# Weight remainders of a two-layer decoder trunk by accumulating transfers instead of GpSimd subtractions

## The chip, the cores and the metric

One core of one Trainium2 chip runs the whole program. The metric is device time in microseconds, from the first to the last instruction of the launch. The kernel before was timed three times: 1368.78, 1369.29 and 1370.32 us, so the median is 1369.29 us.

## The reference

Everything is float32. The sequence has 512 positions of width 1024, and there are two layers. Each layer is a mixer and a SwiGLU feed-forward, and both are wrapped as `x <- LayerNorm(alpha * x + f(x))`:

```python
for layer in range(DEPTH):                                   # DEPTH = 2
    if layer % 2 == 0:
        h = conv_sgu_mixer(x, ...)                           # 1024 -> 2048 in, 1024 -> 1024 out
    else:
        h = dilated_attention_mixer(x, positions, ...)       # 1024 -> 9216 q/k/v, 3 groups x 8 heads x 128
    x = layer_norm(DN_ALPHA * x + h, ln_g[layer, 0], ln_b[layer, 0])
    x = layer_norm(DN_ALPHA * x + swiglu(x, w_gate, w_up, w_down), ln_g[layer, 1], ln_b[layer, 1])

def swiglu(x, w_gate, w_up, w_down):                         # hidden width 2816
    return (jax.nn.silu(x @ w_gate) * (x @ w_up)) @ w_down
```

What matters here is the weights: 236 pieces of 512 KB (128 partitions x 1024 float32), called slabs, are read once each and multiplied with activations that stay on the chip.

## The kernel before

**Products in three passes.** TensorE multiplies in the format fp32r, which keeps fewer bits than float32. To keep float32's precision each factor is split in two: the rounded value (`_hi`) and the remainder (`_lo` = value - rounded value), and a product is made as hi*hi + hi*lo + lo*hi. So each slab of weights needs three things before TensorE can finish with it: its load, its rounded copy and its remainder.

**The ring of slabs.** Loads, rounded copies and remainders each have RING = 4 places; slab n uses place n % 4. The steps of a plain slab are:

- SyncE's queue loads it into `stage` (`load_view`); it waits until the remainder of slab n-4 is made, since that reads the old contents of the place.
- ScalarE (ACT) copies `stage` to `w_hi`, which rounds it (`split_high`, L1201); it waits for the load and until TensorE has used slab n-4 (`w_used`). It then counts up `w_hi_ready`.
- GpSimd (Pool) subtracts, `w_lo = stage - w_hi` (`split_low`, L618); it waits for `w_hi_ready` and counts up `w_lo_ready`.
- TensorE (PE) waits for `w_lo_ready` (`slab_ready`) and multiplies: `columns` (L712 to L714) for q, k and the columns behind a norm, `tokens` (L734 to L736) for down and output projections, L1129 to L1131 for v.

Each of these queues runs in the order in which the code issues, without a planner. ACT's order around the change is written out: a slab's rounding stands in front of other work of that stage, as the rounding of the hidden activations (L1457), the copies of q and k out of PSUM (L1525), of v (L1589) and the exponentials (L1536).

**The stages**, with the slab numbers that the text uses:

| slabs | stage | who makes the remainder before |
|---|---|---|
| 0 to 23 | layer 0, mixer in and out | Pool |
| 24 to 67 | layer 0, gate and up (4 plain ones, then units) | Pool 3 and VectorE 1; units VectorE |
| 68 to 89 | layer 0, down projection | Pool |
| 90 to 161 | layer 1, q, k, v | Pool |
| 162 to 169 | layer 1, output projection | Pool |
| 170 to 213 | layer 1, gate and up | as layer 0 |
| 214 to 235 | layer 1, down projection | Pool |

**Where three slabs are wanted at once.** Down and output projections go slab by slab over all four token tiles (`whole_rows`), 24 products of 512 columns each. The last three slabs go tile by tile instead (`finish_tiles`), so that the LayerNorm of tile 0 can start early. It therefore waits for all three remainders at its start: slabs 87 to 89, 167 to 169 and 233 to 235. The last of the three can be rounded only when slab n-4 has been used, which leaves one slab's products between that and the start of `finish_tiles`.

**Behind a norm** (`columns_behind_norm`) the first four slabs of the next stage are multiplied in two rounds, tokens 0 to 255 of all four and then tokens 256 to 511 of all four, and only the second round releases their places, one every 24 short products. Slab 94 is the first one after the four of layer 1's q and k.

Of the kernel before, what the change touches and what calls it, by code (L numbers as in the profile page):

```python
# [10 lines left out]
ACT = mybir.ActivationFunctionType  # L11
ALU = mybir.AluOpType
# [28 lines left out]
RING = 4  # L41


N_IN, N_OUT, N_UP, N_DOWN, N_ATT = 16, 8, 2 * KF, KF, 72
S_IN = 0
S_OUT0 = S_IN + N_IN
S_UP0 = S_OUT0 + N_OUT
S_DOWN0 = S_UP0 + N_UP
S_ATT = S_DOWN0 + N_DOWN
S_OUT1 = S_ATT + N_ATT  # L50
S_UP1 = S_OUT1 + N_OUT
# [55 lines left out]
def trunk(nc, x, positions, ev_w_in, ev_conv_w, ev_conv_b, ev_conv_ln_g, ev_conv_ln_b, ev_sgu_ln_g,  # L107
# [3 lines left out]
    with ctx:  # L111
        def sb(name, shape, dt=F32, scope=ctx):
            return scope.enter_context(nc.sbuf_tensor(name, shape, dt))

        def sem(name):
            return ctx.enter_context(nc.semaphore(name))
# [6 lines left out]
        w_stage = [stage[:, j, :] for j in range(RING)]  # L123
        w_hi = [sb(f"w_hi{j}", [P, SLAB], F32R) for j in range(RING)]
        w_lo = [sb(f"w_lo{j}", [P, SLAB], F32R) for j in range(RING)]
# [91 lines left out]
        w_loaded = [sem(f"w_loaded{j}") for j in range(RING)]  # L217
        w_hi_ready = sem("w_hi_ready")
        w_lo_ready = sem("w_lo_ready")
        w_used = sem("w_used")  # L220
        x_loaded = [sem(f"x_loaded{i}") for i in range(TILES)]
        ident_loaded = sem("ident_loaded")
# [139 lines left out]
        def plain(slab):  # L362

            return slab - sum(min(max(slab - up - RING, 0), N_UP - RING) for up in (S_UP0, S_UP1))

        def unit_stage(up, par):

            first = (up + 2 * par) % RING
            return stage[:, first, :], stage[:, first + 1, :], stage[:, first:first + 2, :].rearrange(
                "p a (b n) -> p (a b) n", n=512)  # L370
# [53 lines left out]
        def v_slab(turn, k):  # L424

            return S_ATT + turn * TURN_SLABS + QK_SLABS + k
# [85 lines left out]
        def _(sp):  # L512
            def load_view(slab, turns, view):

                slot = slab % RING
                behind_units = [(up // S_UP1, slab - up - N_UP) for up in (S_UP0, S_UP1)
                                if up + N_UP <= slab < up + N_UP + RING]
                if behind_units:
                    layer, j = behind_units[0]
                    sp.wait_ge(d_lo_set if j % 2 else s4_set, layer * UNITS + UNITS - 1 + j // 2)  # L520
                elif slab >= RING:
                    sp.wait_ge(w_lo_ready, plain(slab - RING) + 1 + RING * turns)
                dst = w_stage[slot][:, :].rearrange("p (k n) -> p k n", k=view.shape[1])
                sp.dma_start(dst, view).then_inc(w_loaded[slot], 16)

# [83 lines left out]
        @block.gpsimd  # L609
        def _(pool):  # L610
            pool.memset(ones[:, :], 1.0 / CONV_CH).then_inc(ones_set, 1)
            pool.memset(eps[:, :], EPS).then_inc(ones_set, 1)
            pool.memset(a_pad[:, :, 0:PAD], 0.0).then_inc(pad_set, 1)

            def split_low(slab, turns=0):

                pool.wait_ge(w_hi_ready, plain(slab) + 1 + RING * turns)
                pool.tensor_tensor(w_lo[slab % RING][:, :], w_stage[slab % RING][:, :],  # L618
                                   w_hi[slab % RING][:, :].bitcast(F32), ALU.subtract).then_inc(w_lo_ready, 1)

            def add_shift(e, i):

                for half in range(2):
                    pool.wait_ge(x_scaled, SCALED_PARTS * e + min(2 * i + half + 1, SCALED_PARTS))
                    xh = x_res[:, i, half * 512:(half + 1) * 512]
                    pool.tensor_tensor(xh, xh, norm_b[:, half * 512:(half + 1) * 512], ALU.add).then_inc(x_normed, 1)

            def norm(e, following):

                if e < 3:  # L630
                    split_low(following)
                add_shift(e, 0)
                add_shift(e, 1)
                if e < 3:
                    split_low(following + 1)
                add_shift(e, 2)
                if e < 3:
                    split_low(following + 2)
                    if e in (0, 2):
                        keep_x(e, following)  # L640
                    else:
                        split_low(following + 3)

            def keep_x(e, up):

                pool.wait_ge(w_used, plain(up))
                pool.wait_ge(xt_set, 2 * TILES * (e + 1) + 4)
                for half in range(2):
                    k = slice(half * KH, (half + 1) * KH)
                    pool.tensor_tensor(x_kept[:, k, :], xt_hi[:, k, 0:HALF].bitcast(F32), xt_lo[:, k, 0:HALF].bitcast(F32),  # L650
                                       ALU.add).then_inc(x_kept_set, 1)

            for slab in range(S_UP0):
                split_low(slab)
                if slab == 17:
                    pool.wait_ge(acc_set, 1)
                    pool.wait_ge(chunk_summed, 1)
                    pool.tensor_tensor(tap_sum[:, 0, :], acc[:, 0, :], acc[:, 2, :], ALU.add).then_inc(pair_summed, 1)
                for n, c, w in conv_taps(slab):
                    if w == dve_taps[c]:  # L660
                        continue
                    m = n - 1 - c
                    pool.wait_ge(tap_product, n + 1)
                    if m:
                        pool.wait_ge(tap_added, m)
                    pool.tensor_tensor(tap_sum[:, c, :], tap_sum[:, c, :], mixed[:, m % 2, :], ALU.add
                                       ).then_inc(tap_added, 1)
                    if w == CONV_WIDTH - 1:
                        pool.wait_ge(sum_begun, c + 1)
                        pool.wait_ge(tap_added, m + 1)  # L670
                        pool.tensor_tensor(acc[:, c, :], acc[:, c, :], tap_sum[:, c, :], ALU.add
                                           ).then_inc(chunk_summed, 1)
            norm(0, S_UP0)

            def feed_forward(down, e):
                with pool.Fori(0, N_DOWN // RING) as t:
                    for j in range(RING):
                        split_low(down + j, t)
                for slab in range(down + N_DOWN // RING * RING, down + N_DOWN):
                    split_low(slab)  # L680
                norm(e, down + N_DOWN)

            feed_forward(S_DOWN0, 1)
            with pool.Fori(0, N_ATT // RING - 1) as t:
                for j in range(RING):
                    split_low(S_ATT + RING + j, t)
            for slab in range(S_OUT1, S_UP1):
                split_low(slab)
            norm(2, S_UP1)
            feed_forward(S_DOWN1, 3)  # L690
# [4 lines left out]
        @block.tensor  # L695
        def _(pe):
            def slab_ready(slab, turns=0):
                pe.wait_ge(w_lo_ready, plain(slab) + 1 + RING * turns)

            def columns(slab, bank, tiles=(0, TILES)):  # L700

# [95 lines left out]
            for c in range(CC):  # L797
                slab = S_IN + 2 * c
# [12 lines left out]
            for s in range(4):  # L811
                slab = S_IN + 8 + s
# [20 lines left out]
            for c in range(CC):  # L833
                slab = S_IN + 12 + c
# [355 lines left out]
        def _(act):  # L1190
            def split_high(slab, turns=0):

                act.wait_ge(w_loaded[slab % RING], 16 * (slab // RING + 1) + 16 * turns)
                behind_units = [(up // S_UP1, slab - up - N_UP) for up in (S_UP0, S_UP1)
                                if up + N_UP <= slab < up + N_UP + RING]
                if behind_units:
                    layer, j = behind_units[0]
                    act.wait_ge((a1_used, s12_used, s3_used, d_used)[j], (layer + 1) * UNITS - (j == 3))
                elif slab >= RING:
                    act.wait_ge(w_used, plain(slab - RING) + 1 + RING * turns)  # L1200
                act.activation(w_hi[slab % RING][:, :], w_stage[slab % RING][:, :], ACT.Copy).then_inc(w_hi_ready, 1)  # L1201

            def x_high(e, i):
                for half in range(2):
# [123 lines left out]
            for i in range(TILES):  # L1328
                act.activation(v_tok[:, i, :], v_tok[:, i, :], ACT.Identity, bias=shift[:, i:i + 1],
                               scale=rstd[:, i:i + 1]).then_inc(v_set, 1)  # L1330
# [227 lines left out]
            for turn in range(TURNS):  # L1558
# [20 lines left out]
                for k in range(V_SLABS):  # L1579
                    g, a = divmod(k, 4)  # L1580
                    slab = v_slab(turn, k)
# [64 lines left out]
        def _(dve):  # L1646
# [252 lines left out]
            def feed_forward(layer, up, e):  # L1899
# [3 lines left out]
                def low_plain(slab):  # L1903

                    dve.wait_ge(w_hi_ready, plain(slab) + 1)
                    dve.wait_ge(w_lo_ready, plain(slab))
                    dve.tensor_tensor(w_lo[slab % RING][:, :], w_stage[slab % RING][:, :],
                                      w_hi[slab % RING][:, :].bitcast(F32), ALU.subtract).then_inc(w_lo_ready, 1)

# [362 lines left out]
```

## Time and profile before

| | |
|---|---|
| runs | 1368.78, 1369.29, 1370.32 us; median 1369.29 us |
| profiled execution | span 1369.0 us from its first to its last instruction; nothing else of its time is given |
| TensorE (PE), busy | 1355.4 us, 99% |
| VectorE (DVE), busy | 887.1 us, 65% |
| ScalarE (ACT), busy | 615.3 us, 45% |
| GpSimd (POOL), busy | 451.1 us, 33% |
| DMA | 133.52 MB on SyncE's queue, 33.3% of 16 engines' span |

The shares of the four engines are averages over very different stages. For a change at one point of the ring the columns to look at are the start times of the instructions of one slab on each engine: they tell how long before TensorE wanted a remainder it was there. PE's records are pipelined: one product of 512 columns is shown with 0.39 us, but the next one starts 0.227 us behind it (24 of them make 5.44 us), so starts are read, not durations.

### The profile page before, as it was taken

To read this page: it belongs to the slowest core of one execution; us is meant where nothing else is said; L and a number is where in the kernel's file an instruction comes from. 1 tells how busy PE (TensorE), PEld (TensorE's weight loads), DVE (VectorE), ACT (ScalarE), POOL (GpSimd) and SP (SyncE) were. 2 spreads that over 40 slices of the span, in tenths; PEclk is the share of its full clock that TensorE was granted. 3 is DMA by queue.
4 is the path that set the end of the run, shared out by engine and by line. 5 is a ranking of instruction groups with operands and counts; after the bars stand their busy time and mean duration, and the time that the engine had idled before them with its cause. 6 is when DMAs were issued, how large, how long until landed. Compare 5 with 4: busy or idle time off the path is not lost.

```text
span 1369.0 us, 20672 instructions
## 1 busy us (share of the span) xinstructions
PE 1355.4 (99%) x8121; PEld 1208.5 (88%) x8121; DVE 887.1 (65%) x1122; ACT 615.3 (45%) x959; POOL 451.1 (33%) x218
## 2 busy tenths in 40 slices
PE   8999999999999999999999999999999999999997
PEld 7887899999988889888888888888889999998886
DVE  3997698888856355677433665724159888885445
ACT  4465555555542454333433434434255555554233
POOL 4785600000054454344443332444260000005443
PEclk9999999999999999999999999999999999999999
DMA  9323223343453323332442322254122334335321
GB/s 269 93 94 92 63 78 108 92 122 92 112 167 95 105 62 93 93 93 84 132 124 67 88 82 73 77 164 130 47 62 78 107 92 122 92 113 164 96 74 62
DMA packets 181961, 138.72 MB, mean 101 GB/s; under 512 B 8789, under 2 KB 162153, under 8 KB 181896
## 3 DMA queue, kind: packets, MB, share of 16 engines
q1 hardware_dynamic: 175272, 133.52, 33.3%
q10 hardware_dynamic: 6624, 4.29, 1.3%
q8 instruction: 45, 0.74, 0.2%
q14 instruction: 20, 0.16, 0.0%
HBM read 133.56 MB, written 4.24 MB: 101 GB/s over the span
## 4 chain that ended last, share of the span: by engine, by line
PE 97%; DVE 1%; DMA 1%; ACT 1%; SPq 0%; issue 0%; DVEq 0%
PE pq L940 10%; PE pq L939 10%; PE pq L937 10%; PE pq L712 9%; PE pq L714 9%; PE pq L713 9%; PE pq L734 8%; PE pq L735 8%; PE pq L736 8%; PE pq L1130 3%; PE pq L1131 3%; PE pq L1129 3%; PE pq L1108 1%; PE pq L1067 1%; PE pq L1080 1%; PE pq L1101 1%
## 5 line engine op out<-in xcount | busy, mean ns | idle before, releaser
L618 POOL TENSOR_TENSOR w_lo<-stage,w_hi 128x1024 fp32r<-128x1024 f32 x154 | 374.5, 2441 | 873.9 <-ACT w_hi L1201 873.8
L1201 ACT ACTIVATE w_hi<-stage 128x1024 fp32r<-128x1024 f32 x156 | 161.6, 1056 | 238.2 <-PE pq L736 164.8
L712 PE MATMUL pq<-xt_hi,w_hi 128*128 128x512 f32 (+1 forms) x624 | 228.4, 366 | 0.5 <-DVE xt_lo L1653 0.4
L714 PE MATMUL pq<-xt_hi,w_lo 128*128 128x512 f32 (+1 forms) x624 | 225.2, 361 | 0.0
L713 PE MATMUL pq<-xt_lo,w_hi 128*128 128x512 f32 (+1 forms) x624 | 225.1, 361 | 0.0
L940 PE MATMUL pq<-xt_hi,w_lo 128*128 128x256 f32 x632 | 178.9, 283 | 0.0
L939 PE MATMUL pq<-xt_lo,w_hi 128*128 128x256 f32 x632 | 178.9, 283 | 0.0
L937 PE MATMUL pq<-xt_hi,w_hi 128*128 128x256 f32 x632 | 178.8, 283 | 0.0
L712 PEld LDWEIGHTS pq<-xt_hi,w_hi 128*128 128x128 f32 x624 | 117.9, 189 | 19.5 <-DVE xt_lo L1653 1.2
L714 PEld LDWEIGHTS pq<-xt_hi,w_lo 128*128 128x128 f32 x624 | 117.8, 189 | 18.0
L937 PE MATMUL pq<-xs_hi,w_hi 128*128 128x256 f32 x472 | 133.6, 283 | 0.0
L939 PE MATMUL pq<-xs_lo,w_hi 128*128 128x256 f32 x472 | 133.6, 283 | 0.0
L940 PE MATMUL pq<-xs_hi,w_lo 128*128 128x256 f32 x472 | 133.6, 283 | 0.0
L713 PEld LDWEIGHTS pq<-xt_lo,w_hi 128*128 128x128 f32 x624 | 117.9, 189 | 17.1
L937 PEld LDWEIGHTS pq<-xt_hi,w_hi 128*128 128x128 f32 x632 | 121.3, 192 | 0.1
L939 PEld LDWEIGHTS pq<-xt_lo,w_hi 128*128 128x128 f32 x632 | 121.3, 192 | 0.1
L940 PEld LDWEIGHTS pq<-xt_hi,w_lo 128*128 128x128 f32 x632 | 121.3, 192 | 0.0
L2032 DVE TENSOR_TENSOR xs_lo<-ht,xs_hi 128x512 fp32r<-128x512 f32 x26 | 63.4, 2440 | 67.7 <-ACT xs_hi L1457 67.7
L937 PEld LDWEIGHTS pq<-xs_hi,w_hi 128*128 128x128 f32 x472 | 90.6, 192 | 0.0
L939 PEld LDWEIGHTS pq<-xs_lo,w_hi 128*128 128x128 f32 x472 | 90.6, 192 | 0.0
L940 PEld LDWEIGHTS pq<-xs_hi,w_lo 128*128 128x128 f32 x472 | 90.6, 192 | 0.0
L734 PE MATMUL pq<-w_hi,xs_hi 128*128 128x512 f32 x208 | 81.0, 389 | 0.0
(261 smaller groups left out, 2808.4 us busy)
## 6 DMA issues: line engine op xcount, KB each, us to landing
stage<-in_od_w_qkv_dram SPq DMA_DIRECT2D x72, 512.0 KB, 3.9
stage<-in_ffn_w_gate_dram SPq DMA_DIRECT2D x44, 512.0 KB, 4.9
stage<-in_ffn_w_up_dram SPq DMA_DIRECT2D x44, 512.0 KB, 3.9
stage<-in_ffn_w_down_dram SPq DMA_DIRECT2D x44, 512.0 KB, 3.5
stage<-in_ev_w_in_dram SPq DMA_DIRECT2D x16, 512.0 KB, 5.7
stage<-in_ev_w_out_dram SPq DMA_DIRECT2D x8, 512.0 KB, 3.6
stage<-in_od_w_out_dram SPq DMA_DIRECT2D x8, 512.0 KB, 3.9
x_res<-in_x_dram SPq DMA_DIRECT2D x4, 512.0 KB, 6.2
```

The costliest lines, as they stand in the source:

```text
L618: pool.tensor_tensor(w_lo[slab % RING][:, :], w_stage[slab % RING][:, :], w_hi[slab % RING][:, :].bitcast(F32), ALU.subtract).then_inc(w_l ...
L712: pe.matmul(o, hi[:, k, :], x_hi, start=(k == 0), stop=False)
L713: pe.matmul(o, hi[:, k, :], x_lo, start=False, stop=False)
L714: last = pe.matmul(o, lo[:, k, :], x_hi, start=False, stop=(k == KD - 1))
L734: pe.matmul(o, t_hi[:, tile * P:(tile + 1) * P], hi, start=first, stop=False)
L735: pe.matmul(o, t_hi[:, tile * P:(tile + 1) * P], lo, start=False, stop=False)
L736: return pe.matmul(o, t_lo[:, tile * P:(tile + 1) * P], hi, start=False, stop=end)
L937: pe.matmul(o, hi[:, k, :], x_block[0][:, k, :], start=(first and k == 0), stop=False, skip_group_check=True)
L939: pe.matmul(o, hi[:, k, :], x_block[1][:, k, :], start=False, stop=False, skip_group_check=True)
L940: last = pe.matmul(o, lo[:, k, :], x_block[0][:, k, :], start=False, stop=(k == KH - 1), skip_group_check=True)
L1201: act.activation(w_hi[slab % RING][:, :], w_stage[slab % RING][:, :], ACT.Copy).then_inc(w_hi_ready, 1)
L2032: dve.tensor_tensor(lo, ht[:, k, :], hi.bitcast(F32), ALU.subtract).then_inc(ht_set, 1)
```

## The change

For 120 slabs the remainder is no longer a subtraction on Pool. ACT writes the rounded slab twice, once as before into `w_hi` and once with its sign turned into `w_lo`; only then does it count up `w_hi_ready`. Pool issues a DMA that adds `stage` onto `w_lo` (`accum_op=ALU.add`), from on-chip memory to on-chip memory, 512 KB, so that `w_lo` becomes stage - rounded slab. Its landing is counted on one new semaphore for each place of the ring, and all who waited for `w_lo_ready` of such a slab wait for that: PE's `slab_ready` and SyncE's load of slab n+4.

The 120 slabs are those from the first down projection on (68 to 89, 94 to 169, 214 to 235). The four slabs behind each norm (90 to 93, 170 to 173), everything before slab 68 and the units stay as they are.

```diff
+        w_lo_landed = [sem(f"w_lo_landed{j}") for j in range(RING)]
...
+        def lo_done(slab, turns=0):
+
+            if by_transfer(slab):
+                return w_lo_landed[slab % RING], 16 * sum(by_transfer(n) and not in_units(n) for n in range(slab % RING, slab + 1, RING))
+            return w_lo_ready, sum(not by_transfer(n) and not in_units(n) for n in range(slab + 1)) + turns * RING
...
+        def by_transfer(slab):
+
+            return S_DOWN0 <= slab and not any(n <= slab < n + RING for n in (S_ATT, S_UP1))
...
-                    sp.wait_ge(w_lo_ready, plain(slab - RING) + 1 + RING * turns)
+                    sp.wait_ge(*lo_done(slab - RING, turns))
...
                 pool.wait_ge(w_hi_ready, plain(slab) + 1 + RING * turns)
+                if by_transfer(slab):
+                    pool.dma_start(w_lo[slab % RING][:, :], w_stage[slab % RING][:, :], accum_op=ALU.add
+                                   ).then_inc(lo_done(slab)[0], 16)
+                    return
                 pool.tensor_tensor(w_lo[slab % RING][:, :], w_stage[slab % RING][:, :],
                                    w_hi[slab % RING][:, :].bitcast(F32), ALU.subtract).then_inc(w_lo_ready, 1)
...
-                pe.wait_ge(w_lo_ready, plain(slab) + 1 + RING * turns)
+                pe.wait_ge(*lo_done(slab, turns))
...
-                act.activation(w_hi[slab % RING][:, :], w_stage[slab % RING][:, :], ACT.Copy).then_inc(w_hi_ready, 1)
+                high = act.activation(w_hi[slab % RING][:, :], w_stage[slab % RING][:, :], ACT.Copy)
+                if by_transfer(slab):
+                    high = act.activation(w_lo[slab % RING][:, :], w_stage[slab % RING][:, :], ACT.Copy, scale=-1.0)
+                high.then_inc(w_hi_ready, 1)
```

Pool's loops over the slabs of the down projections and of the attention projections become straight code. On Pool, from the last two instructions of layer 0's first norm to the end of the program, this stands in the queue before (`w_lo<-stage,w_hi` is the subtraction, `x_res<-x_res,norm_b` the adds of the LayerNorm's shift):

```order
L676 UNCONDITIONAL_BRANCH
L676 ISA
L618 TENSOR_TENSOR w_lo<-stage,w_hi 128x1024 [waits w_hi_ready]
L617 REGISTER_ALU
...
L676 COMPARE_AND_BRANCH
L618 TENSOR_TENSOR w_lo<-stage,w_hi 128x1024 [waits w_hi_ready] x3
L626 TENSOR_TENSOR x_res<-x_res,norm_b 128x512 [waits x_scaled] x4
L618 TENSOR_TENSOR w_lo<-stage,w_hi 128x1024 [waits w_hi_ready]
```

and in its place after the change:

```order
L634 DMA w_lo<-stage 128x1024 [waits w_hi_ready] x22
L637 TENSOR_TENSOR w_lo<-stage,w_hi 128x1024 [waits w_hi_ready]
L645 TENSOR_TENSOR x_res<-x_res,norm_b 128x512 [waits x_scaled] x4
L637 TENSOR_TENSOR w_lo<-stage,w_hi 128x1024 [waits w_hi_ready]
L645 TENSOR_TENSOR x_res<-x_res,norm_b 128x512 [waits x_scaled] x2
L637 TENSOR_TENSOR w_lo<-stage,w_hi 128x1024 [waits w_hi_ready] x2
L634 DMA w_lo<-stage 128x1024 [waits w_hi_ready] x76
```

The 22 subtractions of the down projection have become transfers, the four around the norm have stayed where they stood, and the next 76 slabs are transfers again.

On ACT, behind the norm of layer 0 and around slabs 94 and 95, the queue before is (`qk<-pq` copies q or k out of PSUM, `xt_hi<-pq` rounds the turned activations):

```order
L1201 ACTIVATE w_hi<-stage 128x1024 x2
L1206 ACTIVATE xt_hi<-pq 128x16x32 x4
L1525 ACTIVATE qk<-pq 128x512 x2
L1201 ACTIVATE w_hi<-stage 128x1024 x2
L1525 ACTIVATE qk<-pq 128x512 x2
```

and after the change:

```order
L1216 ACTIVATE w_hi<-stage 128x1024 x2
L1224 ACTIVATE xt_hi<-pq 128x16x32 x4
L1543 ACTIVATE qk<-pq 128x512 x2
L1216 ACTIVATE w_hi<-stage 128x1024
L1218 ACTIVATE w_lo<-stage 128x1024
L1216 ACTIVATE w_hi<-stage 128x1024
L1218 ACTIVATE w_lo<-stage 128x1024
L1543 ACTIVATE qk<-pq 128x512 x2
```

The first row (slabs 92 and 93) is unchanged; slabs 94 and 95 take four instructions of ACT instead of two, and slab 95's rounding stands behind slab 94's negated copy.

## Rows read from the trace of the kernel before

**Rows 1.** The page: busy us by engine, and the chain that ended last.

```profile
PE 1355.4 (99%) x8121; PEld 1208.5 (88%) x8121; DVE 887.1 (65%) x1122; ACT 615.3 (45%) x959; POOL 451.1 (33%) x218
...
PE 97%; DVE 1%; DMA 1%; ACT 1%; SPq 0%; issue 0%; DVEq 0%
```

**Rows 2.** PE's waits, 376 to 1369 us: us in total, times, longest.

```profile
PE pq L712 <- DVE xt_lo L1653: 0.2, 1, 0.2
PE pq L712 <- issue: 0.2, 1, 0.2
```

**Rows 3.** The page's groups: busy us, mean ns, idle before.

```profile
L618 POOL TENSOR_TENSOR w_lo<-stage,w_hi 128x1024 fp32r<-128x1024 f32 x154 | 374.5, 2441 | 873.9 <-ACT w_hi L1201 873.8
L1201 ACT ACTIVATE w_hi<-stage 128x1024 fp32r<-128x1024 f32 x156 | 161.6, 1056 | 238.2 <-PE pq L736 164.8
```

**Rows 4.** Timeline (start, us, what), one slab of the down projection, four engines.

```profile
401.58 1.06 ACT L1201 ACTIVATE w_hi<-stage 128x1024 fp32r<-128x1024 f32 x1 [3.86 <-PE pq L736]
402.55 0.61 ACT L1457 ACTIVATE xs_hi<-ht 128x512 fp32r<-128x512 f32 x1
...
402.72 2.40 POOL L618 TENSOR_TENSOR w_lo<-stage,w_hi 128x1024 fp32r<-128x1024 f32 x1 [3.04 <-ACT w_hi L1201]
...
403.19 2.48 DVE L2032 TENSOR_TENSOR xs_lo<-ht,xs_hi 128x512 fp32r<-128x512 f32 x1 [2.96 <-ACT xs_hi L1457]
...
406.76 0.39 PE L734 MATMUL pq<-w_hi,xs_hi 128*128 128x512 f32 x1
```

**Rows 5.** Timeline, slab 89 and the start of `finish_tiles`.

```profile
483.18 1.06 ACT L1201 ACTIVATE w_hi<-stage 128x1024 fp32r<-128x1024 f32 x1 [3.86 <-PE pq L736]
...
488.36 0.39 PE L734 MATMUL pq<-w_hi,hr_hi 128*128 128x512 f32 x1
```

**Rows 6.** Timeline, slab 235 and the start of the last `finish_tiles`.

```profile
1338.81 1.06 ACT L1201 ACTIVATE w_hi<-stage 128x1024 fp32r<-128x1024 f32 x1 [3.86 <-PE pq L736]
...
1343.99 0.39 PE L734 MATMUL pq<-w_hi,hr_hi 128*128 128x512 f32 x1
```

**Rows 7.** Timeline, slabs 94 and 95 on ACT, and slab 94's first product.

```profile
527.27 2.01 ACT L1201 ACTIVATE w_hi<-stage 128x1024 fp32r<-128x1024 f32 x2
...
531.86 0.40 PE L712 MATMUL pq<-xt_hi,w_hi 128*128 128x512 f32 x1
```

**Rows 8.** Timeline, slab 68: ACT, VectorE beside it, Pool, its first product.

```profile
378.78 1.05 ACT L1201 ACTIVATE w_hi<-stage 128x1024 fp32r<-128x1024 f32 x1
...
379.04 0.68 DVE L2032 TENSOR_TENSOR hr_lo<-ht,hr_hi 128x512 fp32r<-128x512 f32 x1
...
379.90 10.41 POOL L618 TENSOR_TENSOR w_lo<-stage,w_hi 128x1024 fp32r<-128x1024 f32 x4 [208.92 <-ACT w_hi L1201]
...
384.97 0.40 PE L734 MATMUL pq<-w_hi,hr_hi 128*128 128x512 f32 x1
```

**Rows 9.** The page's DMA issues: count, KB each, median us to landing.

```profile
stage<-in_ffn_w_down_dram SPq DMA_DIRECT2D x44, 512.0 KB, 3.5
...
v_rows<-v_att ACTq DMA_DIRECT2D x2, 1024.0 KB, 6.6
...
out_dram<-x_res SPq DMA_DIRECT2D x3, 512.0 KB, 2.7
```

**Rows 10.** Four slabs of the down projection: busy us by engine, PEclk, DMA share.

```profile
396.00:418.00 22.00, 22.00 (x99) 18.23 (x98) 11.19 (x10) 6.41 (x9) 9.62 (x4) 1.00 0.31 99
```

**Rows 11.** Timeline, the copies of v out of PSUM behind slab 120.

```profile
672.99 1.06 ACT L1201 ACTIVATE w_hi<-stage 128x1024 fp32r<-128x1024 f32 x1 [2.85 <-issue]
...
674.47 2.29 ACT L1589 ACTIVATE v_att<-pq 128x512 f32<-128x512 f32 x4 [0.42 <-DMA far_rows<-st_far]
...
675.97 0.39 PE L1129 MATMUL pq<-w_hi,xt_hi 128*128 128x512 f32 x1
```

**Rows 12.** Two stretches at the program's start, columns as in Rows 10.

```profile
4.90:11.70 6.80, 3.51 (x28) 2.79 (x27) 2.50 (x4) 3.77 (x7) 1.39 (x1) 1.00 1.03 338
11.70:15.10 3.40, 3.20 (x15) 3.20 (x16) 2.55 (x4) 2.34 (x5) 0.97 (x1) 0.51 1.20 294
```

More of the change, by code:

```diff
@@ L364, in plain, with in_units @@
             return slab - sum(min(max(slab - up - RING, 0), N_UP - RING) for up in (S_UP0, S_UP1))
+        def lo_done(slab, turns=0):
+            if by_transfer(slab):
+                return w_lo_landed[slab % RING], 16 * sum(by_transfer(n) and not in_units(n) for n in range(slab % RING, slab + 1, RING))
+            return w_lo_ready, sum(not by_transfer(n) and not in_units(n) for n in range(slab + 1)) + turns * RING
+        def in_units(slab):
+            return any(up + RING <= slab < up + N_UP for up in (S_UP0, S_UP1))
+        def by_transfer(slab):
+            return S_DOWN0 <= slab and not any(n <= slab < n + RING for n in (S_ATT, S_UP1))
         def unit_stage(up, par):
@@ L675, in feed_forward @@
             def feed_forward(down, e):
[L676 to L679, printed above, removed]
+                for slab in range(down, down + N_DOWN):
                     split_low(slab)
@@ L683, in _ @@
             feed_forward(S_DOWN0, 1)
-            with pool.Fori(0, N_ATT // RING - 1) as t:
-                for j in range(RING):
-                    split_low(S_ATT + RING + j, t)
+            for slab in range(S_ATT + RING, S_OUT1):
+                split_low(slab)
             for slab in range(S_OUT1, S_UP1):
@@ L1905, in low_plain @@
                     dve.wait_ge(w_hi_ready, plain(slab) + 1)
-                    dve.wait_ge(w_lo_ready, plain(slab))
+                    dve.wait_ge(*lo_done(slab - 1))
                     dve.tensor_tensor(w_lo[slab % RING][:, :], w_stage[slab % RING][:, :],
```

## The prediction

> **What bounds the kernel now.** I read the page first. TensorE is busy 99% of the span, and the chain of work that ended last is 97% PE [rows 1]. A busy PE alone proves little, since its records overlap, so the second view is that of PE's waits over the stretch in which the change acts, from the first down projection at 376 us to the end: two waits of 0.2 us each, 0.4 us in all [rows 2]. So from there on the end is set by the number of products times their spacing, and whatever makes remainders faster than TensorE wants them is worth at most 0.4 us. Pool's subtractions are nowhere on that path: Pool sits idle 873.8 us waiting for ACT's rounding [rows 3]. The question is only the opposite one: where is a remainder made so shortly before it is wanted that a slower way of making it shows? That is the third view, the timeline of single slabs.
>
> **What is removed.** 120 subtractions of 2.44 us [rows 3], 293 us of Pool. They are hidden behind PE today, so this is worth nothing by itself. One side effect: VectorE's remainder of the hidden activations takes 2.48 us when it overlaps a Pool subtraction [rows 4] and 0.68 us for the same shape just before Pool starts [rows 8]. It gets shorter.
>
> **What is added on ACT.** 120 negated copies. I price them as the rounding, 1.056 us [rows 3]; a pair of such instructions takes 2.01 us [rows 7]. That is 127 us on an engine that is busy 45%. In the down projections the xs_hi rounding behind it starts 1.0 us later, so VectorE starts at 404.2 instead of 403.19; PE wants the result at 406.76. With 2.48 us it would be there at 406.7, with 0.68 us at 404.9: hidden either way, though by 0.1 us only if VectorE stays slow [rows 4]. Where v is copied out of PSUM the negated copy of slab 120 pushes four copies from 674.47 to about 675.5; the first takes 0.6 and PE wants its bank at 675.97, so about 0.2 us are lost, in each of two turns [rows 11]: 0.4 us. The other work behind the roundings (q and k copies, exponentials) goes later by one or two copies; PE has no wait on any of it today [rows 2], and I cost it at 0, with a bound of 2 us over both layers.
>
> **The new step: ACT, issue, transfer, landing.** For a slab whose rounding starts at A the transfer is issued at A + 2.01 + 0.08 (the 0.08 is what Pool needs today to start behind ACT's end, 402.64 to 402.72 [rows 4]). The room for it is the time from there to PE's first product that needs the slab:
>
> - A slab in mid-projection: 401.58 + 2.09 = 403.67. The product at 406.76 begins the slab two before it [rows 4], so it is wanted at 406.76 + 2 x 5.44 = 417.6. Room 14 us. Nothing to pay.
> - The last slab of three `finish_tiles` (89, 169, 235): 483.18 + 2.09 = 485.27, wanted at 488.36 [rows 5]. Room 3.09 us. The last one is 1338.81 and 1343.99, the same 5.18 us apart [rows 6]; slab 169 repeats it.
> - Slab 94, first behind the four of layer 1's q and k: 527.27 + 2.09 = 529.36, wanted at 531.86 [rows 7]. Room 2.50 us. Slab 95 is rounded behind the negated copy of 94, so its issue is at 531.4, but it is wanted 5.4 us behind 94 plus the scores: room over 7.
> - The first slab of each down projection (68, 214): 378.78 + 2.09 = 380.87, wanted at 384.97 [rows 8]. Room 4.10 us, twice.
>
> So six places out of 120 have less than 4.2 us, and what they cost hangs on one number that the trace does not hold: L, the time from issue to landing of an accumulating transfer of 512 KB within on-chip memory.
>
> **Bounds of L.** From below: a store of 512 KB out of on-chip memory lands in 2.7 us; a load of a down slab in 3.5 us; 1024 KB out of on-chip memory in 6.6 us [rows 9]. The new transfer writes 512 KB but has to read two operands of 512 KB, so its reads are like the 1024 KB row, its write like the smaller ones. The engines' own time for one plain pass of 512 KB is 0.31 x 22 / 4 = 1.7 us [rows 10]. A load plus one further pass is 3.5 + 1.7 = 5.2 us. I take 5.5 us, between that and 6.6 and nearer to the first, because Pool's queue issues none in this trace and may need more before the first byte. Ends: 2.7 us, and 3.5 + 6.6 = 10.1 us if reading and writing do not overlap.
>
> The Trainium skill (DMA: Bandwidth & Descriptors, the anatomy of one DMA on the GpSimd path) gives 2.0 us plus the bytes at 436 GB/s, an estimate of 3.2 us here and of 4.4 us if the second operand is added as a second pass. Collectives: The Full Stack (why ReduceScatter is half of AllGather) says that an add in the transfer costs through its two source reads, not through the adding. By 4.4 us the sum would be 1.9 + 3 x 1.3 + 2 x 0.3 = 6.4 us and the time about 1376 us. No row here shows either.
>
> **The sum.** With L = 5.5: slab 94 waits 3.0 us; three ends of projections 2.4 us each, 7.2; two starts 1.4 each, 2.8. That is 13.0 us. At the first four of the six with loads around (89, 169, 68, 214) a load's 1.7 us of engine time [rows 10] can fall beside the transfer, since the load of slab n+4 now goes out just when slab n has landed; between 0 and 1.7 us each, I take 0.4: 1.6 us. With 0.4 for the v copies the sum is 15.0 us. PE has nothing behind these waits to catch up with, so each one moves the end. Against the profile's own 1369.0 us that is 1384.0 us; the median of the runs is 0.3 us above that span, so I forecast 1384 us.
>
> At the ends of L: with 2.7 only slab 94 is late, by 0.2 us, 1369.5 us. With 6.6 it is 4.1 + 10.5 + 5.0 = 19.6, with full collisions (6.8) 1395 us. With 10.1 it is 7.6 + 21.0 + 12.0 = 40.6, 1410 us.
>
> **Rivals.**
>
> *The transfer is short enough (not slower).* If it lands within about 3.1 us of its issue, all of the six but slab 94 keep their time, as the 2.7 us of a plain store allow [rows 9]. Against it: it reads twice what that store reads. Its place is the start of `finish_tiles`, its price is 0.2 to 0.8 us, and it decides from L below 3.4, where the sum is 0.9 + 0.9 = 1.8 us. Time 1369.5 to 1371 us. A real gain would need PE's spacing to shrink; PE is not waiting, and nothing in these rows ties its spacing to Pool.
>
> *The DMA engines become the bound.* A slab of the down projection takes 5.44 us, its load 1.7 us of all engines [rows 10]. If the accumulate holds them longer than 3.7 us, the ring starves everywhere, not in six places. Twice a plain pass is 3.4 us, close to that, which speaks for it; against it, the ring has 14 us of room, so only a mean rate above 100% counts. With 4.7 us of engine time a slab is 1.0 us late in the 44 down slabs and about 0.3 us in the 76 attention and output slabs (6.1 us each, 531.86 to 995.85): 67 us, 1436 us. If all of the 6.6 us were engine time, some 300 us.
>
> *TensorE's clock falls at each stop.* At the program's start PE was busy 3.51 of 6.80 us, and in the 3.40 us behind that the granted clock was 0.51, the level of 1.2 GHz; before it was 1.00, that of 2.4 GHz [rows 12]. A stop of 3 us is comparable with that idle time. If each of the six stops brought such a stretch, 1.7 us more each: 10 us, 1394 us. Against it: the shortest stops are 1.4 us inside long dense stretches.
>
> **Chances.** The forecast as it stands (L between 4 and 7.5 us, no clock loss, 1374 to 1397 us): 0.62. Clock loss on top: 0.12. DMA engines the bound: 0.10. Transfer short enough: 0.16, most of which is no change (0.13) and 0.03 an unforeseen gain. A measurement of this kernel can tell about 0.2%, 2.7 us, from no change, so slower means above 1372 us: 0.84, the first three cases. The range 1370.5 to 1412 us reaches into the short transfers from L = 3.2 us on, about half of that case, and leaves out 0.08 below and 0.10 above.
>
> **What would show it.** In the profile after: Pool's subtractions down from 154 to 34, ACT up by about 127 us, VectorE's L2032 near 0.7 us. PE's waits list a DMA into w_lo with six long waits, the longest at slab 94, three alike and two shorter; PE's waits on anything else stay below 1 us. Issue to landing of w_lo reads 5.5 us, and the DMA share in the down projections rises from 0.31 to about 0.65. The prediction is wrong if L is under 3.4 us, if PE waits at more than about ten slabs, or if the time changes with no DMA in PE's waits.

## The result and the profile after

The changed kernel takes 1389.59 us (median of 4 runs, 1389.0 to 1393.37) against 1369.03 us before: ratio 1.0153, 95% interval 1.0139 to 1.0168, so it is 20.6 us slower. The forecast was 1384 us, with 1370.5 to 1412 as its range. The profiled execution took 1389.0 us, of which 1387.0 are its span, 18.0 more than the span before.

The page after, busy us by engine and the chain that ended last, beside [rows 1]:

```profile
PE 1360.4 (98%) x8121; PEld 1210.4 (87%) x8121; DVE 764.0 (55%) x1122; ACT 730.0 (53%) x1079; POOL 263.9 (19%) x218
...
PE 92%; DMA 3%; ACT 2%; DVE 1%; issue 1%; SPq 0%; ACTq 0%; DVEq 0%
```

The work moved as intended: Pool 187 us less, VectorE 123 us less, ACT 115 us more. No sum of this kind is the limit. What reached the path is the 3% of DMA in the chain, which had 1% before, and 2% of ACT instead of 1%: at the places named below the negated copy and the transfer stand one behind the other in front of PE (e5). PE's waits from 376 us on (columns: us in total, times, longest), beside [rows 2]:

```profile
PE pq L749 <- DMA w_lo<-stage: 7.3, 4, 2.7
PE pq L749 <- DVE ht L2043: 3.7, 1, 3.7
PE pq L727 <- DMA w_lo<-stage: 2.2, 1, 2.2
PE pq L1144 <- ACT v_att L1607: 0.9, 1, 0.9
PE pq L727 <- DVE xt_lo L1671: 0.2, 1, 0.2
PE pq L727 <- issue: 0.2, 1, 0.2
```

The 0.4 us of before have become 14.5 us. By their times the stops are slab 68 (0.8), 89 (2.1), 94 (2.2), 169 (2.7), 214 (3.7), 235 (1.6), and one behind a copy of v (0.9). That is one at each of the six places of the prediction and no other transfer of the 120. The second line names VectorE for slab 214; experiment e6 shows that this is the transfer too.

One of the stops, slab 89, on ACT, Pool and PE (start, us, what), beside [rows 5]:

```profile
481.69 1.06 ACT L1216 ACTIVATE w_hi<-stage 128x1024 fp32r<-128x1024 f32 x1 [2.91 <-PE pq L751]
482.66 1.05 ACT L1218 ACTIVATE w_lo<-stage 128x1024 fp32r<-128x1024 f32 x1
...
484.00 0.86 POOL L634 DMA_DIRECT2D w_lo<-stage  x1 [4.58 <-ACT w_lo L1218]
...
486.64 0.39 PE L751 MATMUL pq<-w_hi,hr_lo 128*128 128x512 f32 x1
489.15 0.47 PE L749 MATMUL pq<-w_hi,hr_hi 128*128 128x512 f32 x1 [2.11 <-DMA w_lo<-stage]
```

ACT's pair takes 2.0 us, Pool issues 0.3 us behind it, and PE goes on 5.15 us behind the issue. The step from one product to the next is 2.51 us instead of 0.23.

How long a transfer takes from issue to landing, all 120 (the first line below) and that of slab 94, with no load beside it (the second):

```profile
DMA to landing us min/median/max: 4.5/6.0/11.4
...
DMA to landing us min/median/max: 4.5/4.5/4.5
```

And the stretches in which TensorE's granted clock was at half rate, with the program's start in front and a stretch of the down projection at the end (columns: busy us by engine, PEclk, DMA share, GB/s), beside [rows 10, 12]:

```profile
11.70:15.10 3.40, 3.40 (x31) 3.40 (x30) 1.61 (x3) 2.66 (x4) 1.45 (x1) 1.00 1.18 286
490.20:493.60 3.40, 3.40 (x10) 2.62 (x9) 0.00 (x0) 0.00 (x0) 0.44 (x1) 0.50 0.78 205
538.00:541.40 3.40, 3.40 (x9) 2.63 (x9) 2.70 (x4) 2.76 (x3) 1.61 (x2) 0.50 1.10 235
1254.80:1258.20 3.40, 2.86 (x7) 2.31 (x8) 1.80 (x3) 2.20 (x3) 0.86 (x1) 0.50 1.03 175
396.00:462.00 66.00, 66.00 (x293) 54.67 (x292) 16.13 (x44) 34.42 (x46) 10.34 (x12) 1.00 0.89 200
```

The three stretches at 0.50 begin just behind the stops at 89 and 94 and at the end of that at 214. In the first two PE starts 8 products in 3.4 us where it starts 15 at full rate (x10 and x9 also count products that only reach into the stretch). Read from the starts of the same products in both traces, the three cost 1.6, 1.6 and 1.3 us, 4.5 us in all. The first line goes the other way: at the program's start this execution had no half-rate stretch, the profiled one of before had one [rows 12], and the changed kernel runs 2.6 us ahead from there. The unusual one of the two is the execution of before: its span was 1369.0 us, while 23 others of the same kernel, run beside e1, had spans of 1366.4 to 1368.4 us, median 1366.8. So the span's 18.0 us are 14.1 us of new waits, 4.5 us of clock and about 2.0 us of late first products behind the stops and small shifts, less 2.6 us at the start. Without these 2.6 us the difference is 20.6 us, as the runs have it.

### The profile page after: what moved, and what is told of

Read it like the earlier page. It is cut to its first block, busy times and chain, and to the rows that moved or that the text cites. A ratio compares the mean times of both kernels' runs of the same rounds, so it can differ in the third digit from the quotient of the medians.

```text
span 1387.0 us, 20627 instructions
## 1 busy us (share of the span) xinstructions
PE 1360.4 (98%) x8121; PEld 1210.4 (87%) x8121; DVE 764.0 (55%) x1122; ACT 730.0 (53%) x1079; POOL 263.9 (19%) x218
## 3 DMA queue, kind: packets, MB, share of 16 engines
q1 hardware_dynamic: 175272, 133.52, 32.1%
q0 software_dynamic: 17280, 62.92, 25.5%
## 4 chain that ended last, share of the span: by engine, by line
PE 92%; DMA 3%; ACT 2%; DVE 1%; issue 1%; SPq 0%; ACTq 0%; DVEq 0%
PE pq L955 9%; PE pq L954 9%; PE pq L952 9%; PE pq L727 9%; PE pq L729 9%; PE pq L728 9%; PE pq L749 8%; PE pq L751 8%; PE pq L750 8%; PE pq L1144 3%; PE pq L1146 3%; PE pq L1145 3%; DMA w_lo<-stage 2%; PE pq L1123 1%; PE pq L1082 1%; PE pq L1095 1%
## 5 line engine op out<-in xcount | busy, mean ns | idle before, releaser
L634 POOL DMA_DIRECT2D w_lo<-stage x120 | 104.9, 874 | 1014.5 <-ACT w_lo L1218 994.5
L1216 ACT ACTIVATE w_hi<-stage 128x1024 fp32r<-128x1024 f32 x156 | 164.9, 1059 | 186.8 <-PE pq L751 129.9
L1218 ACT ACTIVATE w_lo<-stage 128x1024 fp32r<-128x1024 f32 x120 | 126.2, 1052 | 0.0
L637 POOL TENSOR_TENSOR w_lo<-stage,w_hi 128x1024 fp32r<-128x1024 f32 x34 | 82.3, 2427 | 55.3 <-ACT w_hi L1216 55.3
```

Of the source, the lines that this page charges most:

```text
L634: pool.dma_start(w_lo[slab % RING][:, :], w_stage[slab % RING][:, :], accum_op=ALU.add).then_inc(lo_done(slab)[0], 16)
L1216: high = act.activation(w_hi[slab % RING][:, :], w_stage[slab % RING][:, :], ACT.Copy)
L1218: high = act.activation(w_lo[slab % RING][:, :], w_stage[slab % RING][:, :], ACT.Copy, scale=-1.0)
```

## The experiments

Nine kernels, each an edit of the changed kernel. Ratios are against runs of the kernel before on the same chip.

### e1: the six slabs back on Pool

```diff
-            return S_DOWN0 <= slab and not any(...)
+            return slab not in (S_DOWN0, S_ATT - 1, S_ATT + RING, S_UP1 - 1, S_DOWN1, N_SLABS - 1) and S_DOWN0 <= slab and not any(...)
```

> The changed kernel with six slabs (68, 89, 94, 169, 214, 235) given back to Pool; the other 114 remainders are still transfers. Theory (the loss is six landings behind PE's need, plus the half-clock stretches that follow such stops): about 1370 us, PE waits for no DMA into w_lo, one wait of 0.9 us on a v copy may stay, no half-clock stretch between the start and the end of the program. Rival A (the extra 127 us of ACT work costs): stays 5 us or more above before. Rival B (the DMA engines are near full and slow everything): stays above 1380 us, with PE waits at other slabs.

Measured: 1371.03 us, ratio 1.0010 (1.0001 to 1.0019). 114 transfers are left, and 19 of the 20.6 us are gone; 1.8 us are left. PE's waits:

```profile
PE pq L1144 <- ACT v_att L1607: 0.7, 1, 0.7
PE pq L727 <- DVE xt_lo L1671: 0.2, 1, 0.2
PE pq L727 <- issue: 0.2, 1, 0.2
```

No wait on a transfer of the ring, and the granted clock is 1.00 from 15 us to 1363 us. ACT is still busy 722.8 us (before: 615.3), and the DMA share in the down projection is still 0.87. Both rivals fall: neither ACT's extra work nor nearly full DMA engines costs more than those 1.8 us by itself.

### e2: the negated copies without the transfers

```diff
+        def negated(slab):
+            return S_DOWN0 <= slab and not any(...)
...
         def by_transfer(slab):
+            return False
...
-                if by_transfer(slab):
+                if negated(slab):
                     high = act.activation(w_lo[...], w_stage[...], ACT.Copy, scale=-1.0)
```

> ACT writes the 120 negated copies as in the changed kernel, but every remainder is Pool's subtraction, which overwrites them; no transfer. Theory: the negated copies alone cost 0.9 to 1.5 us (the v copies), and up to 0.2 us per down slab if VectorE's slow remainder of the hidden activations (2.48 us beside Pool) now ends behind PE's need: 1370 to 1376 us. Rival A (ACT's work is the loss): near 1389 us. Rival B: 1369 to 1371 us, as no transfer is left.

Measured: 1368.96 us, ratio 0.9999 (0.9990 to 1.0008), under the expected 1370 to 1376. The 120 copies cost nothing that can be measured, and PE has no wait on a v copy. All its waits from 376 us on:

```profile
PE pq L731 <- issue: 0.2, 1, 0.2
PE pq L731 <- DVE xt_lo L1675: 0.2, 1, 0.2
```

So ACT's copy in front of the v copies does not make PE wait by itself.

### e3: only the six slabs as transfers

```diff
-            return S_DOWN0 <= slab and not any(...)
+            return slab in (S_DOWN0, S_ATT - 1, S_ATT + RING, S_UP1 - 1, S_DOWN1, N_SLABS - 1)
```

> Only the six slabs 68, 89, 94, 169, 214, 235 are transfers, the other 114 are Pool's. Theory: most of the loss is back, less what neighbouring transfers add by sharing the engines: waits of 2.1 (94), 1.5 to 2.0 (three ends), 0.6 to 1.5 (two starts), about 9.5 us, and some 1.6 us for each of about three half-clock stretches: 1378 to 1386 us, centre 1382. Issue to landing 4.5 us, 5 with a load beside it. Rivals A and B (ACT's total work, full DMA engines): 1370 us or less.

Measured: 1381.57 us, ratio 1.0091 (1.0076 to 1.0107), in the middle of what was expected. PE's waits:

```profile
PE pq L749 <- DMA w_lo<-stage: 7.5, 4, 2.6
PE pq L727 <- DMA w_lo<-stage: 2.2, 1, 2.2
PE pq L749 <- DVE hr_lo L2050: 0.8, 1, 0.8
```

Six transfers out of 120 bring 12.3 of the 20.6 us, and the other 114 by themselves 1.8 (e1). So 6.5 us come only when both are there. Beside the 114 the six land later: the stops at 89, 169 and 214 are 1.7, 1.6 and 2.6 us here and 2.1, 2.7 and 3.7 us in the changed kernel, all six together 10.5 and 13.2 us. And this trace has one half-rate stretch, behind slab 94, where the changed kernel's has three. (The third line is slab 68's stop; for the engine named there, see e6.)

### e4: the three last slabs before a norm back on Pool

```diff
+            return slab not in (S_ATT - 1, S_UP1 - 1, N_SLABS - 1) and S_DOWN0 <= slab and not any(...)
```

> The changed kernel with the three last slabs before a norm or the end (89, 169, 235) given back to Pool. Theory, if the places add: the waits of 2.1, 2.7 and 1.6 us and one half-clock stretch of 1.6 us go, 1389.6 - 8.0 = 1381.6 us; PE still waits at 68, 94 and 214. Rivals A and B: no change from 1389.6 us by so few slabs.

Measured: 1378.12 us, ratio 1.0065 (1.0050 to 1.0079), 3.5 us lower than expected. The three stops are gone, and those at 68, 94 and 214 are there (0.8, 2.2 and 2.5 us). The one at 214 is 1.2 us shorter, the wait on the v copy 0.6 us longer (1.5 us). The profiled execution had no half-rate stretch at all, not behind 94 and 214 either, where the changed kernel had one each; these two I had left in my expectation. It was one of the two short executions of the four (1376.91 us; the others 1376.83, 1379.34 and 1379.55), so how much clock a removed stop gives back is not shown by it.

### e5: the negated copy first

```diff
-                high = act.activation(w_hi[...], w_stage[...], ACT.Copy)
                 if by_transfer(slab):
-                    high = act.activation(w_lo[...], w_stage[...], ACT.Copy, scale=-1.0)
-                high.then_inc(w_hi_ready, 1)
+                    act.activation(w_lo[...], w_stage[...], ACT.Copy, scale=-1.0).then_inc(w_neg_ready, 1)
+                act.activation(w_hi[...], w_stage[...], ACT.Copy).then_inc(w_hi_ready, 1)
```

Pool waits for `w_neg_ready` before it issues; PE and SyncE wait for `w_hi_ready` as well as for the landing.

> The changed kernel with ACT's two copies of a transferred slab in the other order: the negated one first, and the transfer issued on it, the rounded one behind. If the path of the six places is ACT, issue, landing, PE, each issue comes 0.95 us earlier and the waits fall from 14.1 us in all to about 8.6 us (68: 0; 89: 1.2; 94: 1.3; 169: 1.8; 214: 2.8; 235: 0.7; v copy 0.9), and some half-clock stretches go with them: 1381 to 1384.5 us. If the sharing of the DMA engines decides alone, the order on ACT changes little: 1388 us or more.

Measured: 1384.42 us, ratio 1.0101 (1.0083 to 1.0120). The gain of 5 us is the size expected, though the four runs spread from 1380.23 to 1386.17 us. The stops: 89 1.8 us, 94 1.2, 169 1.9, 214 2.4, 235 0.8, five of the six shorter by 0.3 to 1.3 us. Slab 68's grew from 0.8 to 1.4 us, which was expected to vanish: its landing took 6.1 us here instead of 4.7. The wait on a v copy grew too, from 0.9 to 1.6 us. In all PE waits 11.2 us instead of 14.1 for transfers and v copies, so ACT's negated copy is part of the path at these places.

### e6: the LayerNorm loads later

```diff
-                load(first)
-                load(first + 1)
+                for slab in range(first, first + 8):
+                    load(slab)
                 load_ln(e, layer, 1)
-                for slab in range(first + 2, first + N_DOWN):
+                for slab in range(first + 8, first + N_DOWN):
                     load(slab)
```

> The changed kernel with the two LayerNorm parameter loads of 512 KB (norm_g, norm_b) issued behind the eighth slab load of each down projection instead of behind the second. If slab 214's landing (7.6 us behind its issue instead of 4.5) is long because these two and the slab loads are in flight beside it, its wait falls from 3.7 to about 1.3 us and slab 68's from 0.8 to 0.5, with perhaps one half-clock stretch less: 1384.5 to 1387.5 us. If the wait at 214 is VectorE's product of the last unit, as the view of waits has it, nothing changes: 1389.6 us.

Measured: 1387.10 us, ratio 1.0136 (1.0121 to 1.0152), 2 us less than the changed kernel, but the two intervals overlap; the trace is clearer. Slab 214's issue to landing, in the changed kernel (first line) and here (second):

```profile
DMA to landing us min/median/max: 7.6/7.6/7.6
...
DMA to landing us min/median/max: 4.5/4.5/4.5
```

and its stop fell from 3.7 to 0.6 us (here put down to the transfer), with VectorE untouched. The wait that the view gave to VectorE's `ht` was the landing, 1255.2 us by its semaphore; VectorE's product ended 0.1 us later and so came last among the semaphores that the view looked at. That PE does not need that product there is seen in this run, where PE goes on before VectorE has begun it. VectorE in the changed kernel, then PE and VectorE here:

```profile
1254.62 0.69 DVE L2043 TENSOR_TENSOR ht<-pq,gate 128x512 f32<-128x512 f32 x1 [3.96 <-ACT gate L1466]
...
1254.23 0.47 PE L749 MATMUL pq<-w_hi,hr_hi 128*128 128x512 f32 x1 [0.58 <-DMA w_lo<-stage]
...
1255.19 0.69 DVE L2043 TENSOR_TENSOR ht<-pq,gate 128x512 f32<-128x512 f32 x1 [2.52 <-ACT gate L1466]
```

Slab 68's stop stayed at 0.8 us, where I had expected 0.5.

### e7: one more transfer for each slab

```diff
                     pool.dma_start(w_lo[...], w_stage[...], accum_op=ALU.add).then_inc(lo_done(slab)[0], 16)
+                    pool.dma_start(spill[slab % RING], w_stage[slab % RING][:, :]).then_inc(w_spilled[slab % RING], 16)
...
                     sp.wait_ge(*lo_done(slab - RING, turns))
+                    if by_transfer(slab - RING):
+                        sp.wait_ge(w_spilled[slab % RING], lo_done(slab - RING)[1])
```

This is e1 with a store of each of its 114 slabs to device memory added; nothing reads `spill`.

> The kernel with six slabs on Pool (1371.0 us), with one more transfer for each of the 114: Pool also writes the staged slab to a scratch in device memory, which nothing reads, and the next load of the place waits for both. This tells how near the engines are to being the bound. A down slab then needs 2.8 + 1.7 + 1.5 = 6.0 us of all engines against 5.44 us of products: about 0.6 us late for most of the 44 down slabs less what the ring lends, 1385 to 1400 us, DMA share 1.0 in the down projections and PE waits at slabs of mid-projection. If only latency at the six places ever matters: 1371 to 1373 us.

Measured: 1383.82 us, ratio 1.0109 (1.0094 to 1.0125). The time lies just below the range that I expected, but for another reason. The down projection (columns as above) and PE's waits:

```profile
396.00:462.00 66.00, 66.00 (x293) 54.67 (x292) 16.57 (x45) 36.16 (x47) 17.32 (x25) 1.00 1.05 306
...
PE pq L1149 <- ACT v_att L1612: 9.9, 2, 5.5
```

PE does not wait in the down projections at all, at a DMA share of 1.05: the share adds up the times of packets, and one above 1 says that some of these times overlap, so 1.0 is not a bound. I had treated it as one, in the expectation and in the rival of the prediction. The whole loss is at the v copies: two stops of 5.5 and 4.4 us, and a half-rate stretch of 6.8 us that begins in the last 1.0 and 2.2 us of each.

### e8: slab 94 alone

```diff
-            return S_DOWN0 <= slab and not any(...)
+            return slab == S_ATT + RING
```

> Slab 94 alone is a transfer, all else is Pool's. One stop of 2.2 us and nothing else: 1371.2 us if TensorE's clock stays up behind it, 1373 us if a half-clock stretch follows in most executions.

Measured: 1373.71 us, ratio 1.0038 (1.0024 to 1.0051): the second branch. PE around the stop, and the granted clock over it and behind it:

```profile
529.46 0.28 PE L729 MATMUL pq<-xt_hi,w_lo 128*128 128x256 f32 x1
532.11 0.77 PE L727 MATMUL pq<-xt_hi,w_hi 128*128 128x512 f32 x1 [2.38 <-DMA w_lo<-stage]
```

```profile
529.40:531.90 2.50, 0.34 (x3) 0.13 (x2) 2.47 (x2) 2.13 (x4) 1.33 (x2) 0.99 0.84 157
531.90:535.30 3.40, 3.19 (x8) 2.54 (x9) 3.33 (x4) 2.13 (x2) 3.40 (x2) 0.50 0.64 187
```

One stop of 2.4 us, then 3.4 us at half rate. By the medians the kernel is 5.1 us slower than before, twice the wait; in the trace the stop and the stretch behind it cost 4.1 us.

### e9: the slabs of v on Pool too

```diff
+            return not any(0 <= slab - S_ATT - turn * TURN_SLABS - QK_SLABS < V_SLABS for turn in range(TURNS)) and slab not in (S_DOWN0, ...) and ...
```

> The kernel with six slabs on Pool (1371.0 us), with the 24 slabs of v (114 to 125 and 150 to 161) given back to Pool as well; 90 are transfers. If the remaining PE wait on a v copy (0.7 us) comes from ACT waiting for the small transfers far_rows, which land in 3.3 us beside the slab transfers and in 1.7 us before the change, they land in under 2 us again and the wait is gone: 1369.3 us, no different from before. If something else of the transfers costs, it stays at 1370.5 to 1371 us.

Measured: 1369.71 us, ratio 1.0005 (0.9996 to 1.0014). The wait on the v copy is gone. The landings of the small transfers `far_rows` (4 KB each), before, in e1, in e7 and here, in that order:

```profile
DMA to landing us min/median/max: 1.5/1.7/2.8
...
DMA to landing us min/median/max: 2.8/3.3/4.9
...
DMA to landing us min/median/max: 4.9/6.9/7.7
...
DMA to landing us min/median/max: 1.5/1.7/2.7
```

PE's wait on v goes with them: 0, 0.7, 9.9 and 0 us. In e2, with every negated copy and no transfer, they land as before (1.5/1.7/1.8). How the one hangs on the other is seen on ACT in the changed kernel:

```profile
679.33 1.06 ACT L1216 ACTIVATE w_hi<-stage 128x1024 fp32r<-128x1024 f32 x1 [2.53 <-issue]
680.29 1.04 ACT L1218 ACTIVATE w_lo<-stage 128x1024 fp32r<-128x1024 f32 x1
682.51 0.40 ACTq L1627 DMA_DIRECT2D far_nat<-far_rows  x1
682.95 2.07 ACT L1607 ACTIVATE v_att<-pq 128x512 f32<-128x512 f32 x4 [1.61 <-DMA far_rows<-st_far]
```

The two copies of the slab end at 681.3 us. The next transfer in ACT's queue reads `far_rows` and is held until they have landed, and the v copies stand behind it.

With 90 of the 120 remainders made by transfers the kernel is as fast as before, and no faster. No run here is faster than before, which fits the 0.4 us that PE had to give.

## Why the prediction was right, point by point

**The bound, right.** PE's 0.4 us of waits said that freeing Pool could gain at most that. Pool lost 187 us, VectorE's remainder of the hidden activations fell to 0.69 us as forecast, and e9 and e2 with and without all this come out at the time of before.

**The six places, right.** The rooms of 2.5, 3.1 and 4.1 us picked 68, 89, 94, 169, 214 and 235 out of 120. In the trace after, the time from Pool's issue to the point where PE has nothing else to do is 2.4 us at 94, 3.0 at 89, 169 and 235, and 4.0 at 68 and 214, as reckoned. e1 takes the six away and 19 us with them, e3 has only the six and brings 12.3 us.

**L, near in the mean and mis-sized in its parts.** I took 5.5 us everywhere and 0.4 us for a load beside it. At 94 and 235, with no load beside it, it is 4.5 us, so 94 cost 2.2 instead of 3.0 us and 235 1.6 instead of 2.4. At 68, 89, 169 and 214 it is 4.7, 5.0, 5.6 and 7.6 us, so they cost 0.8 instead of 1.8, 2.1 instead of 2.8, 2.7 instead of 2.8, and 3.7 instead of 1.8, each with the collision. The sum of waits at the six was put at 14.6 us and is 13.2 us. That it is so near is partly luck: five places were put 3.3 us too high in all and 214 1.9 us too low. The longest wait was to be at 94 and is at 214, beside the two LayerNorm loads that I had not thought of (e6). The estimate from the Trainium skill, 4.4 us with two passes (DMA: Bandwidth & Descriptors, the anatomy of one DMA on the GpSimd path), agrees with the 4.5 us of a transfer alone; used for all six it would have given a sum of 6.4 us, since it leaves out both the neighbours and the clock.

**The clock, the step that failed.** I made it a rival with 0.12 and costed it at 0 in the sum, because the shortest stops are only 1.4 us inside dense stretches. In the profiled execution three of seven stops had a half-rate stretch, 4.5 us, and e8 shows one behind a stop of 2.4 us alone: 5.1 us by the medians for 2.4 us of waiting. This term is most of the 5.6 us between forecast and result; the waits were 0.9 us under the forecast, and about 2.0 us are late first products and small shifts, which the sum did not have (at slab 89 the step from product to product grew by 2.28 us for a wait of 2.11). So the case that came true is the one with a chance of 0.12, in part of its size, and not the forecast as it stands with its 0.62, whose 1374 to 1397 us hold the time all the same.

**The base, right by two slips.** I added the sum to the profile's span of 1369.0 us, plus 0.3 us to get to the median of the runs. A run's time is about 2 us above its span (1389.0 and 1387.0 us), and the span that I used was 2.2 us longer than the usual one of that kernel. The two cancel.

**The v copies, small as forecast but for the wrong reason.** I had 0.4 us from ACT's extra copy in front of them. e2 has those copies and no wait. The wait of 0.9 us comes from ACT waiting for the landing of `far_rows`, small transfers that take 3.2 us in the changed kernel instead of 1.7 (e1, e7 and e9 move the two together). That wait of ACT was there before the change, 0.42 us in front of the v copies [rows 11], and I had not looked at who else uses the DMA engines.

**The DMA share, wrong.** Forecast 0.65 in the down projections, measured 0.89. I had counted one plain pass for the new transfer; its own share over the program is 25.5% of 1387 us for 120, so 2.9 us each, and a load still has its 1.7 (SyncE's queue has 32.1% of the span, and had 33.3%): 4.6 / 5.44 = 0.85. The rival that hangs on it did not come, and e7 shows that even 1.05 was no bound.

**Left open.** Whether a stop brings a half-rate stretch is not settled by its length alone: in e4 stops of 2.2 and 2.5 us had none and in the changed kernel one of 2.7 us (slab 169), while in e5 one of 1.8 us (slab 89) and in e8 one of 2.4 us had. At which load the down projections do become late was not found.

## What to carry to other kernels

When one engine's products are the bound, list for each buffer how long before its use it is ready, and price a slower way of filling it only at the entries with less room than it needs: here returning six of 120 brought back 19 of the 20.6 us, though the six alone cost only 12.3. Price such a stop at more than its length where it may bring TensorE's clock down, up to twice. And before adding a stream of large transfers, look for the small ones that an engine waits for: here those of 4 KB landed later, and the v copies waited for them.

## What the runs showed of the hardware

- An accumulating transfer of 512 KB within on-chip memory, issued by Pool, lands in 4.5 us with nothing beside it (slab 235); over all 120 the median is 6.0 us and the longest 11.4. Its issue holds Pool for 0.86 us in the median.
- A VectorE subtraction with both inputs in on-chip memory takes 0.69 us for 128x512 alone and 2.48 us beside a Pool subtraction; beside Pool's transfers it takes 0.69 us in all 44 cases.
- Stops of TensorE of 1.8 to 3.7 us were followed by 3.4 us at the granted clock 0.50 in nine cases, and stops of 1.9 to 2.7 us were not in others; stops of 5.5 and 4.4 us went with 6.8 us of it each.
- A DMA share of 1.05 and 306 GB/s over 66 us of a down projection cost that stretch nothing, while the landing of 4 KB transfers in the same kernel rose from 1.7 to 6.9 us.
